# Activations stationary in the output projection and the feed-forward layers, with the residual held by tokens

## What is computed

```
h = rms_norm(x, mix_norm[0]); proj = h @ ab_w_in          # 2048 x 7168
o_a = gated linear recurrence (8 heads); o_b = stick-breaking attention (8 heads)
x = x + concat(o_a, o_b) @ ab_w_out                       # 2048 x 2048
x = x + swiglu(rms_norm(x, ffn_norm[0]), w_gate, w_up, w_down)    # 2048 x 5632 twice, 5632 x 2048
h = rms_norm(x, mix_norm[1]); pooled = (window mean - self), 4 channel groups, windows 2, 4, 8, 16
x = x + (pooled @ pool_w[g] for each group) * pool_scale  # 4 x 512 x 512
x = x + swiglu(rms_norm(x, ffn_norm[1]), ...)
out = rms_norm(x, final_norm)
swiglu(h, g, u, d) = (silu(h @ g) * (h @ u)) @ d
```

## Time and profile before

| | |
|---|---|
| runs | 2024.07, 2024.29, 2025.35 us, median 2024.29 |
| span of the profiled execution | 2023.6 us (its own time beside the span is not listed; the fastest run is 0.5 above it) |
| busy in that span | PE 99%, PEld 86%, DVE 64%, ACT 43%, POOL 5% |
| DMA | 361.5 MB, 179 GB/s on the mean |
| granted PE clock, mean | 0.997 |

### The profile page before, as it was taken

How to read it: one execution, slowest core, us unless ns; L and a number is a source line. 1 busy time by engine, 2 the same in 40 slices (tenths; PEclk the granted TensorE clock), 3 DMA queues, 4 the chain that set the end, 5 groups by cost and what they waited for, 6 DMA issues and landing times.

```text
span 2023.6 us, 28999 instructions
## 1 busy us (share of the span) xinstructions
PE 2001.9 (99%) x11499; PEld 1743.7 (86%) x11499; DVE 1297.0 (64%) x1174; ACT 880.0 (43%) x755; POOL 96.8 (5%) x121
## 2 busy tenths in 40 slices
PE   7999999999999999999999999999999999999997
PEld 6888888888888888888888888888888888888886
DVE  6656788888666555656555688656555666555664
ACT  6444434445444334443344465544433444334453
POOL 1000000005000000000000033000000000000012
PEclk9999999999999999999999999999999999999998
DMA  8555444455555555556555465555555555555552
GB/s 281 171 170 169 148 150 157 149 187 184 183 189 178 189 188 184 181 187 187 185 186 187 150 203 179 174 188 180 189 188 183 181 189 179 190 184 188 169 164 80
DMA packets 352790, 361.52 MB, mean 179 GB/s; under 512 B 5745, under 2 KB 349922, under 8 KB 352482
## 3 DMA queue, kind: packets, MB, share of 16 engines
q1 hardware_dynamic: 352738, 360.79, 55.4%
HBM read 358.67 MB, written 2.10 MB: 178 GB/s over the span
## 4 chain that ended last, share of the span: by engine, by line
PE 98%; DVE 0%; DMA 0%; POOL 0%; ACT 0%; SPq 0%; issue 0%; ACTq 0%; POOLq 0%
PE main L1121 62%; PE main L1123 31%; PE aux L1213 1%; PE aux L1128 0%; PE main L1298 0%; PE main L1300 0%; PE main L1299 0%; DMA vrows<-in_hg_out_norm 0%; PE aux L1315 0%; POOL work L435 0%; PE aux L1152 0%; PE aux L1316 0%; PE aux L1153 0%; PE aux L1225 0%; PE aux L1151 0%; PE aux L1195 0%
## 5 line engine op out<-in xcount | busy, mean ns | idle before, releaser
L1121 PE MATMUL main<-act,hi 128*128 128x512 f32 x3712 | 1317.0, 400 | 4.3 <-DVE lo L733 4.3
L733 DVE TENSOR_TENSOR lo<-raw,hi 128x2048 fp32r<-128x2048 f32 x348 | 797.0, 2291 | 400.5 <-ACT hi L468 399.3
L1123 PE MATMUL main<-act,lo 128*128 128x256 f32 x3712 | 1041.7, 281 | 0.0
L468 ACT CAST hi<-raw 128x2048 fp32r<-128x2048 f32 x348 | 664.8, 1911 | 623.1 <-PE main L1123 623.1
L1121 PEld LDWEIGHTS main<-act,hi 128*128 128x128 f32 x3712 | 698.3, 188 | 176.6 <-issue 5.4
L1123 PEld LDWEIGHTS main<-act,lo 128*128 128x128 f32 x3712 | 701.7, 189 | 0.9 <-issue 0.7
L1121 PE MATMUL main<-mid,hi 128*128 128x512 f32 x1664 | 588.0, 398 | 0.0
L1123 PE MATMUL main<-mid,lo 128*128 128x256 f32 x1664 | 466.2, 280 | 0.0
L1121 PEld LDWEIGHTS main<-mid,hi 128*128 128x128 f32 x1664 | 312.6, 188 | 76.8 <-issue 0.2
L1123 PEld LDWEIGHTS main<-mid,lo 128*128 128x128 f32 x1664 | 314.0, 189 | 0.2 <-issue 0.2
L468 ACT COPY cross<-main 128x512 f32<-128x512 f32 x116 | 68.1, 587 | 429.8 <-PE main L1123 429.8
(11 more groups left out here) (121 smaller groups left out, 439.2 us busy)
## 6 DMA issues: line engine op xcount, KB each, us to landing
raw<-in_ffn_w_gate SPq DMA_DIRECT2D x88, 1024.0 KB, 5.1
raw<-in_ffn_w_up SPq DMA_DIRECT2D x88, 1024.0 KB, 5.1
raw<-in_ffn_w_down SPq DMA_DIRECT2D x64, 1024.0 KB, 5.4
raw<-in_ab_w_in SPq DMA_DIRECT2D x56, 1024.0 KB, 5.1
raw<-in_ffn_w_down SPq DMA_DIRECT2D x32, 768.0 KB, 4.7
raw<-in_ab_w_out SPq DMA_DIRECT2D x16, 1024.0 KB, 5.4
raw<-in_pool_w SPq DMA_DIRECT2D x4, 1024.0 KB, 5.1
work<-in_x SPq DMA_DIRECT2D x2, 1024.0 KB, 6.0
```

The source lines that it names most:

```text
L468: return nc.scalar.copy(out_, in_)
L733: V.tensor_tensor(lo[:, s.place, :], raw[:, s.place, :], hi[:, s.place, :].bitcast(F32), ALU.subtract).then_inc(lo_ready, 1)
L1121: mm(bank(job)[:, c, :], hi[:, s.place, at:at + P], rhs[:, k0 + n, :, :], start=(first and n == 0), stop=False)
L1123: ins = mm(bank(job)[:, c, TOKENS:], lo[:, s.place, at:at + P], rhs[:, k0 + n, 0, :], start=False, stop=(last and n == depth - 1))
```

## The change

In the output projection and the feed-forward layers the roles are exchanged: the activation tile becomes stationary and 512 columns of weights move (`wide`). A slot is now 4 row tiles of 512 columns; the PE first makes all 16 products of the rounded weights (as soon as `hi` is ready), then the 8 of the remainders (after `lo`). The pool mixer's products go through the same function. Results lie with tokens on partitions, so the residual `xn` is kept by tokens, both terms of a product land in the same columns, the norm's factor is a value per partition (ACT's square sums a row itself; POOL's additions and the PE's means go), and `pool_scale` and `final_norm` come as rows broadcast to all partitions (`across`, two loads). What is contracted next must be transposed: `turn_wide` makes 8 transposes of 128 x 128, `take_hi` (ACT) and `take_lo` (DVE) bring them into `act` or `mid`. Units are twice as wide, `UNITS = (4, 4, 3)`; the loops of these layers on SP, ACT, DVE and PE are written out. The two feed-forward layers now have 8 x 11 gate and up slots and 4 x 11 down slots each.

```diff
-UNITS = (8, 8, 6)
+UNITS = (4, 4, 3)
+WIDE = 512
-        xT = sb("xT", [P, DT, TOKENS])
+        xn = sb("xn", [P, 2, D])
...
+            def wide_rows(w, row, col):
+                return w[row:row + WIDE, col:col + WIDE].rearrange("(k p) c -> p k c", p=P)
+            sp.wait_ge(hg_out, PAIRS)
+            sp.dma_start(across, pool_scale[0].partition_broadcast(P)).then_inc(scale_loaded, 16)
...
+                    for u in range(u0, u0 + n):
+                        for part, w in enumerate((w_gate, w_up)):
+                            for k in range(4):
+                                load(Count(s0 + 8 * (u - u0) + 4 * part + k),
+                                     wide_rows(w[layer], WIDE * k, WIDE * u), 4)
+                    for m in range(4):
+                        for i in range(n):
+                            load(Count(s0 + 8 * n + n * m + i),
+                                 wide_rows(w_down[layer], WIDE * (u0 + i), WIDE * m), 4)
...
+            def take_hi(k, dst, gain):
+                sc.wait_ge(turned, k + 1)
+                if gain is None:
+                    copy(dst, aux[:, 2:4, :].rearrange("p b (d t) -> p (b d) t", t=TOKENS)).then_inc(turn_hi, 1)
+                    return
+                for d in range(4):
+                    ins = nc.scalar.mul(dst[:, d, :], aux[:, 2 + d // 2, (d % 2) * TOKENS:(d % 2 + 1) * TOKENS],
+                                        vecs[:, gain + d:gain + d + 1])
+                ins.then_inc(turn_hi, 1)
+            def square(norm, m):
+                for h in range(2):
+                    need(sc, sq_done, 8 * (norm - 1) + 2 * m + h)
+                    nc.scalar.activation(squares, xn[:, h, WIDE * m:WIDE * (m + 1)], ACT.Square,
+                                         accum_out=ssq[:, h, m:m + 1]).then_inc(sq_done, 1)
+            def gate_root(s, job, u):
+                sc.wait_ge(slot_used, s + 1)
+                for h in range(2):
+                    norm = N_FFN0 if job < J_FFN1 else N_FFN1
+                    sigmoid(sig[:, h, :], bank(Count(job))[:, h, :], norms[:, norm, h:h + 1]).then_inc(gate_sig, 1)
...
-            def add_residual(s, job, pair_no):
+            def add_residual(s, job, m):
                 need(ve, slot_used, s + 1)
-                xs = xT[:, both(pair_no), :]
-                for half in range(2):
-                    ps = bank(job)[:, :, half * TOKENS:(half + 1) * TOKENS]
-                    ins = V.tensor_tensor(xs, xs, ps, ALU.add)
-                    if half == 0:
-                        chain.link(ins)
-                        chain.settle()
-                ins.then_inc(job_emptied, 1)
+                xs = xn[:, :, WIDE * m:WIDE * (m + 1)]
+                V.tensor_tensor(xs, xs, bank(job), ALU.add).then_inc(job_emptied, 1)
+            def take_lo(k, dst, gain):
+                ve.wait_ge(turn_hi, k + 1)
+                if gain is None:
+                    V.tensor_tensor(dst[:, :, 1, :], aux[:, 2:4, :].rearrange("p b (d t) -> p (b d) t", t=TOKENS),
+                                    dst[:, :, 0, :].bitcast(F32), ALU.subtract).then_inc(turn_taken, 1)
+                    return
+                for d in range(4):
+                    ins = V.scalar_tensor_tensor(dst[:, d, 1, :],
+                                                 aux[:, 2 + d // 2, (d % 2) * TOKENS:(d % 2 + 1) * TOKENS],
+                                                 vecs[:, gain + d:gain + d + 1], dst[:, d, 0, :].bitcast(F32),
+                                                 ALU.mult, ALU.subtract)
+                    if d < 3:
+                        chain.link(ins)
+                ins.then_inc(turn_taken, 1)
+            def gate_out(job, u, norm):
+                for h in range(2):
+                    ve.wait_ge(gate_sig, 2 * u + h + 1)
+                    ins = V.scalar_tensor_tensor(hid[:, h, :], bank(job)[:, h, :], norms[:, norm, h:h + 1],
+                                                 sig[:, h, :], ALU.mult, ALU.mult)
+                    if h == 0:
+                        chain.link(ins)
+                ins.then_inc(job_emptied, 1)
+            def up_out(s, job, norm):
+                need(ve, slot_used, s + 1)
+                need(ve, job_emptied, job)
+                chain.settle()
+                for h in range(2):
+                    ins = V.scalar_tensor_tensor(hid[:, h, :], bank(job)[:, h, :], norms[:, norm, h:h + 1],
+                                                 hid[:, h, :], ALU.mult, ALU.mult)
+                    if h == 0:
+                        chain.link(ins)
+                ins.then_inc(job_emptied, 1)
+            def keep_z(g):
+                s, job = Count(S_POOL + g), Count(J_POOL + g)
+                need(ve, slot_used, s + 1)
+                need(ve, mix_done, g - 1)
+                for h in range(2):
+                    ins = V.scalar_tensor_tensor(zt[g % 2][:, h, :], bank(job)[:, h, :],
+                                                 norms[:, N_MIX1, h:h + 1], across[:, WIDE * g:WIDE * (g + 1)],
+                                                 ALU.mult, ALU.mult)
...
+            def mix_in(g):
+                ve.wait_ge(mix_done, g + 1)
+                xs = xn[:, :, WIDE * g:WIDE * (g + 1)]
+                V.tensor_tensor(xs, xs, aux[:, 0:2, :], ALU.add).then_inc(x_mixed, 1)
...
+            def wide(s, job, lhs, k0, first, last):
+                if first:
+                    need(pe, job_emptied, job - 1)
+                pe.wait_ge(hi_ready, s + 1)
+                at = s % RING
+                for c in range(2):
+                    for h in range(2):
+                        o = bank(Count(job))[:, h, :]
+                        for n in range(4):
+                            w_hi = hi[:, at, n * WIDE:(n + 1) * WIDE]
+                            mm(o, lhs[:, k0 + n, c, h * P:(h + 1) * P], w_hi,
+                               start=(first and c == 0 and n == 0), stop=False)
+                pe.wait_ge(lo_ready, s + 1)
+                for h in range(2):
+                    o = bank(Count(job))[:, h, :]
+                    for n in range(4):
+                        w_lo = lo[:, at, n * WIDE:(n + 1) * WIDE]
+                        ins = mm(o, lhs[:, k0 + n, 0, h * P:(h + 1) * P], w_lo, start=False,
+                                 stop=(last and n == 3))
+                ins.then_inc(slot_used, 1)
+            def turn_wide(k, src):
+                need(pe, turn_taken, k)
+                for d in range(4):
+                    for h in range(2):
+                        at = (d % 2) * TOKENS + h * P
+                        ins = turn(aux[:, 2 + d // 2, at:at + P], src[:, h, d * P:(d + 1) * P])
+                ins.then_inc(turned, 1)
+            def turn_hidden(layer, u, job):
+                pe.wait_ge(job_emptied, job + 1)
+                turn_wide(T_HIDDEN[layer] + u, hid)
...
                 for g, (s0, j0, u0, n) in enumerate(ffn_groups(s_ffn, j_ffn)):
+                    for i in range(n):
+                        first = u0 + i == 0
+                        for b in range(8):
+                            if first and b < 4:
+                                pe.wait_ge(turn_taken, (T_OUT, T_MIX)[layer] + b + 1)
+                            wide(s0 + 8 * i + b, j0 + 2 * i + b // 4, act, 4 * (b % 4), b % 4 == 0, b % 4 == 3)
+                            if b == 0 and i > 0:
+                                turn_hidden(layer, u0 + i - 1, j0 + 2 * i - 1)
...
+                    for m in range(4):
+                        for i in range(n):
+                            if m == 0:
+                                pe.wait_ge(turn_taken, T_HIDDEN[layer] + u0 + i + 1)
+                            wide(s0 + 8 * n + n * m + i, j0 + 2 * n + m, mid, 4 * i, i == 0, i == n - 1)
+                            if m == 0 and i == 0:
+                                turn_hidden(layer, u0 + n - 1, j0 + 2 * n - 1)
+                            if last and layer == 0 and m > 0 and i == 0:
+                                pe.wait_ge(job_emptied, j0 + 2 * n + m)
+                                turn_xn(T_POOL + m - 1, m - 1)
```

More of the change, by code:

```diff
@@ L368, in _ @@
[L368 to L374, removed]
-                            load(Count(s0 + 4 * n + j - 4, 4, i),
-                                 block_rows(w_down[layer], (2 * u0 + n * half) * P, n,
-                                            i * (2 * COLS) + (m - 2) * COLS), n)
@@ new lines, in take_hidden, with take_x, sum_rows, invert @@
+            def take_hidden(layer, u, u_local):
+                take_lo(T_HIDDEN[layer] + u, mid[:, 4 * u_local:4 * u_local + 4, :, :], None)
+            def take_x(k, m, gain):
+                take_lo(k, act[:, 4 * m:4 * m + 4, :, :], gain + 4 * m)
+            def sum_rows(norm):
+                ve.wait_ge(sq_done, 8 * norm)
+                V.tensor_reduce(norms[:, norm, :], ssq[:], AX.X, ALU.add).then_inc(row_sum, 1)
+            def invert(norm):
+                ve.wait_ge(row_rms, norm + 1)
```

(41 more changed lines are left out.)

638 lines of the change are left out of this document (237 added, 401 removed).

## The result

The changed kernel takes 1989.45 us (median of 4 runs, 1988.88 to 1990.08), the kernel before took 2024.82 in the same comparison: ratio 0.9826, 95% interval 0.9812 to 0.984. That is 35.4 us off; forecast were 1991.7 and -32.6.

What follows compares the result with a forecast made beforehand. The PE was taken as the bound; -56.2 + 29.6 + 1.0 - 5.7 + 0.5 - 0.5 - 1.3 = -32.6 took the span from 2023.6 to 1991.0, median 1991.7 us; own range 1984 to 1998, eight in ten 1983 to 2012.

Steps and rivals of the forecast that it cites:

- What bounds: Whole kernel: the PE is the bound, busy 2001.9 of 2023.6 us; neither `lo` nor memory is late.
- Part 1: Output projection and feed-forward products: same columns, 24 instructions a slot for 32, 1580.3 to 1524.1 us, so -56.2 us.
- Part 2: PE between slots: 34 turns of 8 transposes at 0.87 us, +29.6, and slower steps after them, +1.0.
- Part 3: Work leaving the PE: means over partitions, a row mean, small fp32 instructions, output-row transposes; -5.7 us.
- the pool waits: Pool stage: PE waits because ACT and DVE have extra work beside the splits; +0.5 us charged (0 to 3).
- Part 4: DVE, ACT, POOL, DMA: new handoffs stay off the path while ahead of the PE; only +0.5 us, in the pool stage.
- Part 5: Head and tail: the first `lo` starts earlier, -0.5 us; the work after the last product shortens, -1.3 us.
- The slow beat after the change: Rival: wide products stay at 0.2311 us, 2020 throughout, 2005 at half of the turns, 2034 at 0.2333; 9%.
- Cost by columns: Rival: product cost goes by columns, not instructions, so the slots keep 1580 us and the kernel takes 2048; 3%.
- New waits: Rival: PE waits at its turns for takers or `up_out` queued behind splits; 2060 us at 2 us each; 5%.
- Straight-line code: Rival: unrolled loops of these layers starve the PE; 2020 us at 0.1 us per slot; 3%.

Runs made afterwards that it cites:

- a_half: Changed kernel with each product of 512 columns made as two of 256 into the halves of the same bank: 2079.2 us, ratio 1.0269.
- b_wait: Kernel before with each weights-stationary slot's products grouped, all of 512 columns before those of 256, `lo` still awaited at the slot's start: 2001.4 us, ratio 0.9887.
- a_mixalt: Changed kernel, each wide slot's 8 remainder products made as 16 of 256 columns, each behind a rounded one, `lo` awaited at the start: 2040.64 us, ratio 1.0081.
- a_mixgrp: Changed kernel, each wide slot's 8 remainder products made as 16 of 256 columns, all after the 16 rounded ones: 2023.84 us, ratio 0.9997.
- b_order: Kernel before, all weights-stationary slots with 512-column products first, then those of 256, `lo` awaited only before the latter: 1998.69 us, ratio 0.9869.
- a_turn2: Changed kernel with each of the 34 turns made twice, 16 transposes for 8: 2019.8 us, ratio 0.9974.
- a_order: Changed kernel with its 56 attention and recurrence slots grouped, 512-column products first, then 256, `lo` awaited in the middle: 1986.28 us, ratio 0.9814.

## Why the prediction was right, and where its reason was short

*What bounds.* Right: the PE before and after. Behind the first slot the changed kernel's PE waits for nothing, and the PE before waited once, 0.4 us for POOL in the pool mixer.

*Part 1, the products, -56.2.* The size was right: 280 slots at 5.44 to 5.45 us. The reason was half of it. I wrote that each product costs 13 ns beside its columns "and in the feed-forward pairs 17; the change issues a quarter fewer", and took the 17 as something that goes with the count. The runs split it. The cost of a product is 13.2 ns (a_half); 280 x 8 fewer are 29.6 us. The other 26 to 27 are the slow beat, which hangs on the alternation of 512 and 256 columns: grouping alone gives 23.3 without a product fewer (b_wait), the alternation brought back costs 16.8 (a_mixalt against a_mixgrp). I had seen both beats in the trace and named the slow one as a rival for the products *after*, without asking what makes it *before*. The number came out right all the same, because both spacings were read from rows and the sum needs only their difference, not its cause; a forecast of b_order by the same reason missed by 25 us.

The Trainium skill's fixed cost of a warm product, 2.5 ns ("TensorE: Matmul & The Clock Gate", Back-to-back issue gap), stood against the change. The section gives it for the gap of a single product and not for a stream in which each product has its own weight load, which is what both kernels are. a_half measured 13.2 for such a stream of float32r products, so the 2.5 doesn't hold here; had it held, the change would have lost, by the prediction's estimate (6 us for the products against 30 for the turns).

*Part 2, the turns, +29.6 and +1.0.* Right: 0.9 us each by the timeline, 0.89 by a_turn2.

*Part 3, what leaves, -5.7.* No run measures it by itself. An estimate from the two traces, each group with the slower steps around it: two means at 0.89, the row mean 1.27 with its wait for POOL, seven groups of output rows at 0.45, `mix` 2.6 for 2.7 four times; together -6.6. Parts 1 to 3 with the pool waits were to give -30.8; the stages from the output projection to the last product give -32.9. Of the 2.1 between, 0.5 are the pool waits that did not come and 0.9 are this part; 0.7 stay open.

*Part 4, the handoffs.* Right that nothing waits. The +0.5 for the pool stage was not used: `mix_in(0)` there is done at 1229.64 and the PE's turn begins at 1230.18 (rows below), 0.5 us of cover where I had 0.2 too little; the four scaled copies of ACT take 1.56 us, not the 2.2 that I had summed.

```profile
1228.42 1.22 DVE L966 TENSOR_TENSOR xn<-xn,aux 128x1024 f32<-128x1024 f32 x1
```

```profile
1230.18 1.04 PE L1080 MATMUL aux<-ident,xn 128*128 128x128 f32 x8
```

*Part 5.* Head -0.7 for -0.5, tail -0.7 for -1.3.

*What was not in the sum:* -1.1 us in the attention and recurrence stages, whose instructions are the same on the PE. More of their alternating slots run at the quick beat: what their pairs take above 0.3467 adds up to 3.2 us before and 2.2 after. Where these slots are grouped the difference is gone: behind the first slot the stages take 359.0 us in b_order and 359.1 in a_order, against 361.3 before and 360.2 after. So it is the beat; why more slots fall into the quick one is not shown. It varies between versions of the changed kernel too: in six traces of kernels that have these stages alike they take 359.5 to 360.2.

*The rivals.* The slow beat after the change: each turn is followed by slower steps within its first 3 to 10 products and then by 0.227, never by more, while in a_mixalt, with the second length, most slots behind a turn are slow; these steps are the 0.1 us in the slot behind a turn. Cost by columns: fell (a_half). New waits: none, even with the turns doubled. Straight-line code: the PE runs it without a gap, though the bytes of instructions fetched went from 0.61 to 1.13 MB.

So the change takes the slow beat away twice over, by its order and by its equal lengths. From before, in steps that were run: grouping -23.3 (b_wait, 2001.4); then the form with tokens on partitions, its turns and the same 32 products +22.4 (a_mixgrp, 2023.8); then 24 products for 32, -34.4 (1989.45). Weights stationary with grouped products (b_order, 1998.7) has three quarters of the gain for a change of a few lines.

## What to carry to other kernels

Where the PE is busy all the time, read the distance between starts, by length of product, and count what it is above the columns' own time: here 13 ns, 6% of a product of 512 columns and 11% of one of 256. Fewer and longer products pay that back, and transposes spend it, so count both in the same unit. If two lengths alternate, try first to group them; it adds no product (a grouped slot took 5.57 us, an alternating one 5.55 or 5.65 by its beat), and a change that also makes the lengths equal will otherwise be credited with it.

## What the runs showed of the hardware

- A float32r product, each with its own weight load, costs 13.2 ns beside its columns at the 2.4 GHz level, at 256 columns (starts 0.120 apart) as at 512 (0.227). At 256 columns in a row the starts stay 0.120 apart although a weight load is recorded with 0.192 us (a_half): the loads too start 0.120 apart, so one is still recorded as running when the next begins.
- An alternation of 512 and 256 columns has two beats, 0.3467 and 0.3533 for a pair. In the kernel before the slow one held for some 730 us on end and the quick one for some 77; a group of plain fp32 instructions between them can switch it. What in the PE keeps the beat stays open. At one length the stream is back at 0.227 within ten products.
- At the start of the program the granted clock is not the same in every run: two traces of one kernel have 0.50 and 1.00 (14.9 to 17.5 us) and first slots of 7.22 and 5.67 us.
